# Second block of a two-block model on Trainium2: x kept token-major, norms per token tile

## The reference, cut to what matters

```python
def rmsnorm(x, g):
    xf = x.astype(jnp.float32)
    y = xf * lax.rsqrt(jnp.mean(xf * xf, axis=-1, keepdims=True) + EPS)
    return (y * g.astype(jnp.float32)).astype(x.dtype)

# end of the first block, layer 1
x = x + g2[:, None, :] * hier_moe(h, ...)      # 16 experts, 2 of them per token

for l in range(DEPTH):                         # second block, DEPTH = 2
    h = rmsnorm(x, norm_mix_pre[l])
    proj = h @ w_in[l]                         # retention, short conv, long conv, gates
    ...
    merged = gates[:, :, 0] * y_ret + gates[:, :, 1] * y_sc + gates[:, :, 2] * y_cf
    x = x + rmsnorm(merged @ w_o[l], norm_mix_post[l])

    h = rmsnorm(x, norm_ffn_pre[l])
    up = causal_dwconv(h @ w_up[l], ffn_conv_w[l])
    gate, val = jnp.split(up, 2, axis=-1)      # 2816 features each
    f = (jax.nn.silu(gate) * val) @ w_down[l]
    x = x + rmsnorm(f, norm_ffn_post[l])
```

## Time and profile before

| | us |
|---|---|
| median of 3 runs | 3486.62 (3484.47 to 3488.95) |
| the profiled execution, its own time | 3486.04 |
| its span, first to last instruction | 3484.3 |
| TensorE busy (matmul) | 3043.4, 87% of the span |
| VectorE busy | 2129.5, 61% |
| ScalarE busy | 1261.6, 36% |
| POOL busy | 466.0, 13% |
| mean granted TensorE clock | 0.932 |

### The profile page before, as it was taken

The page is one execution under the profiler, slowest core; times in us unless marked ns, Lnnn a source line. Parts: engine busy times, 40 slices in busy tenths (PEclk is TensorE's granted clock), DMA queues, the critical chain, the costliest instruction groups (busy, mean ns, idle before and its releaser), DMA issues. The chain is left out here.

```text
span 3484.3 us, 32354 instructions
## 1 busy us (share of the span) xinstructions
PE 3043.4 (87%) x12460; PEld 2334.5 (67%) x12460; DVE 2129.5 (61%) x2371; ACT 1261.6 (36%) x1417; POOL 466.0 (13%) x118
## 2 busy tenths in 40 slices
PE   2699698887888787999899996999969999969997
PEld 2334476665767665777677874787858777758876
DVE  5544779978788845997565743665055565266621
ACT  3224257643211113886322233443132223234422
POOL 1100100002400010000000002344410000124432
PEclk9879899998989897999999998999989999989998
DMA  4200459962200002996221221222222222212221
GB/s 189 109 0 23 171 217 412 412 239 97 88 10 22 16 25 73 350 361 254 101 85 62 97 85 61 85 96 85 96 79 97 73 85 85 85 52 97 98 91 60
DMA packets 87148, 420.01 MB, mean 121 GB/s; under 512 B 9651, under 2 KB 14899, under 8 KB 58732
## 3 DMA queue, kind: packets, MB, share of 16 engines
q1 hardware_dynamic: 81260, 376.32, 29.8%
q10 hardware_dynamic: 5760, 41.95, 3.1%
HBM read 416.14 MB, written 2.10 MB: 120 GB/s over the span
## 5 line engine op out<-in xcount | busy, mean ns | idle before, releaser
L221 PE MATMUL psum<-h_high,weights_low 128*128 128x512 f32 x2016 | 799.8, 397 | 58.3 <-DVE h_low L340 56.6
L184 POOL TENSOR_TENSOR weights_low<-weights_raw,weights_high 128x2048 fp32r<-128x2048 f32 x99 | 461.1, 4657 | 2883.3 <-ACT weights_high L180 2883.3
L222 PE MATMUL psum<-h_high,weights_high 128*128 128x512 f32 x2016 | 793.8, 394 | 0.0
L223 PE MATMUL psum<-h_low,weights_high 128*128 128x512 f32 x2016 | 792.9, 393 | 0.0
L180 ACT ACTIVATE weights_high<-weights_raw 128x2048 fp32r<-128x2048 f32 x167 | 319.7, 1915 | 801.5 <-PE psum L223 750.1
L221 PEld LDWEIGHTS psum<-h_high,weights_low 128*128 128x128 f32 x2016 | 384.7, 191 | 159.2 <-issue 78.4
L222 PEld LDWEIGHTS psum<-h_high,weights_high 128*128 128x128 f32 x2016 | 384.3, 191 | 81.3 <-issue 1.4
L223 PEld LDWEIGHTS psum<-h_low,weights_high 128*128 128x128 f32 x2016 | 384.0, 190 | 81.2
L340 DVE TENSOR_TENSOR weights_low<-weights_raw,weights_high 128x2048 fp32r<-128x2048 f32 x68 | 155.8, 2292 | 280.1 <-ACT weights_high L180 280.1
L1329 DVE TENSOR_TENSOR weights_low<-more_raw,weights_high 128x1024 fp32r<-128x1024 f32 x168 | 202.0, 1220 | 13.2 <-ACT weights_high L1000 8.5
L1000 ACT ACTIVATE weights_high<-more_raw 128x1024 fp32r<-128x1024 f32 x168 | 178.5, 1062 | 71.1 <-PE psum L1146 32.9
(11 more groups left out here) (410 smaller groups left out, 4726.3 us busy)
## 6 DMA issues: line engine op xcount, KB each, us to landing
weights_raw<-in_moe SPq DMA_DIRECT2D x168, 512.0 KB, 5.9
more_raw<-in_moe SPq DMA_DIRECT2D x168, 512.0 KB, 6.2
weights_raw<-in_w_mix SPq DMA_DIRECT2D x68, 1024.0 KB, 4.8
weights_raw<-in_w_up SPq DMA_DIRECT2D x44, 1024.0 KB, 4.8
mod_weights<-in_ada_w ACTq DMA_DIRECT2D x40, 1024.0 KB, 8.0
weights_raw<-in_w_down SPq DMA_DIRECT2D x22, 1024.0 KB, 4.9
weights_raw<-in_hy_w_in SPq DMA_DIRECT2D x12, 1024.0 KB, 4.8
mod_weights<-in_ada_w SPq DMA_DIRECT2D x8, 1024.0 KB, 15.8
```

The source lines that it names most:

```text
L184: self.nc.gpsimd.tensor_tensor(self.low[:, g % 2, :], self.raw[:, g % 2, :], self.high[:, g % 2, :].bitcast(F32), ALU.subtract).then_inc(s ...
L221: nc.tensor.matmul(out, w[1], rhs[0], start=start, stop=False)
L222: nc.tensor.matmul(out, w[0], rhs[0], start=False, stop=False)
L223: return nc.tensor.matmul(out, w[0], rhs[1], start=False, stop=stop)
```

## The change

From the last expert phase on, x is token-major: `m.X` has 128 tokens on the partitions, and `token_tile(m, t)` is the 1024 features of token tile t. The expert return, the output projection and ffn-down take a token tile as the stationary operand and stream the weights (or expert results), so their PSUM result is token-major too, two banks for each of four token tiles. The norms then sum along the free axis, per tile, with `accum_out`, and the root is one number for each partition. `tail_act`, `tail_pe` and `tail_dve` do, tile by tile, the norm behind the projection, the residual, the next norm, the transposes of h back to feature-major, and its high and low parts; the norms at the head of `phase_mix` and `phase_ffn_up` are gone. The gains come as rows of 1024, spread over the partitions, by DMA (`load_rows`). In the expert phase x is flipped by 32 transposes, and the gate is spread to a row by 8 matmuls, within the routing. The ScalarE step that makes the next phase's first high part stands behind `tail_act` there. The last phase stores each token tile as it is ready. The loops of `phase_ffn_down` are unrolled, and buffers are laid out anew (`moe_front`, `Gs`, `hT`).

```diff
+            if pre is not None:
+                load_rows(sp, s, pre_row, (pre,))
...
+            def x_tokens(first, end):
+                for c in range(first, end):
+                    act.wait_ge(s.x_flip, c + 1)
+                    nc.scalar.activation(m.X[:, c, :], m.psum[:, c % 4, :], ACT.Copy).then_inc(s.x_token, 1)
+            if pre is not None:
+                x_tokens(0, 4)
             act.wait_ge(s.m2, 1)
             nc.scalar.activation(EL[:, 1, :, :], EL[:, 1, :, :], ACT.Exp).then_inc(s.e2, 1)
+            if pre is not None:
+                x_tokens(4, KC)
+                act.wait_ge(s.gate_spread, 1)
+                nc.scalar.activation(gate_row[:, :], token_psum(m, 3), ACT.Copy).then_inc(s.gate_out, 1)
             highs(2)
             for c in range(KC):
                 act.wait_ge(s.gathered, c + 1)
...
+            if pre is not None:
+                tail_act(nc, act, m, s, post=False)
             if following is not None:
...
+            if pre is not None:
+                pe.wait_ge(s.tok_low, KC)
+                for c in range(KC):
+                    if c >= 4:
+                        pe.wait_ge(s.x_token, c - 3)
+                    for t in range(TT):
+                        mm = nc.tensor.transpose(m.psum[:, c % 4, t * P:(t + 1) * P], m.X[:, c, t * P:(t + 1) * P],
+                                                 m.const("ident"))
+                    mm.then_inc(s.x_flip, 1)
+                pe.wait_ge(s.m1, 1)
+                for c in range(KC):
+                    mm = nc.tensor.matmul(token_psum(m, 3)[:, c * P:(c + 1) * P], gate[:, c:c + 1].broadcast_to([P, P]),
+                                          m.const("ident"), start=True, stop=True)
+                mm.then_inc(s.gate_spread, 1)
...
+            def back_tokens(t, slots):
+                for half in range(2):
+                    for k in slots:
+                        for y in (xl, xh):
+                            mm = nc.tensor.matmul(m.psum[:, 2 * t + half, :], rows[:, k, t * P:(t + 1) * P],
+                                                  y[:, k, 4 * half:4 * half + 4, :].rearrange("p c n -> p (c n)"),
+                                                  start=(k == 0 and y is xl), stop=(k == SLOTS - 1 and y is xh))
+                return mm
             pe.wait_ge(s.slot_rows, 1)
             pe.wait_ge(s.y_ready, SLOTS - 1)
+            if pre is not None:
+                for t in range(2):
+                    back_tokens(t, range(SLOTS - 1))
+                pe.wait_ge(s.y_ready, SLOTS)
+                for t in range(2):
+                    back_tokens(t, range(SLOTS - 1, SLOTS)).then_inc(s.y_tile, 1)
+                for t in range(2, TT):
+                    back_tokens(t, range(SLOTS)).then_inc(s.y_tile, 1)
+                tail_pe(nc, pe, m, s)
+                return
             for c in range(4):
                 back(c, c, range(SLOTS - 1))
...
+def token_tile(m, t):
+    return m.X[:, :, t * P:(t + 1) * P]
...
+def tail_y_root(nc, act, m, s, t):
+    act.wait_ge(s.y_tile, t + 1)
+    nc.scalar.activation(m.hT[:, t, :], token_psum(m, t), ACT.Square, accum_out=m.stats[:, t:t + 1]).then_inc(s.y_summed, 1)
+    act.wait_ge(s.y_summed, t + 1)
+    nc.scalar.activation(m.stats[:, 4 + t:5 + t], m.stats[:, t:t + 1], ACT.Sqrt, bias=m.const("eps"), scale=1.0 / D)\
+        .then_inc(s.y_root, 1)
+def tail_x_root(nc, act, m, s, t):
+    act.wait_ge(s.x_ready, t + 1)
+    nc.scalar.activation(by_feature(m.hT[:, t, :]), token_tile(m, t), ACT.Square, accum_out=m.stats[:, 8 + t:9 + t])\
+        .then_inc(s.x_summed, 1)
+    act.wait_ge(s.x_summed, t + 1)
+    nc.scalar.activation(m.stats[:, 12 + t:13 + t], m.stats[:, 8 + t:9 + t], ACT.Sqrt, bias=m.const("eps"), scale=1.0 / D)\
+        .then_inc(s.x_root, 1)
...
+def tail_high(nc, act, m, s, t):
+    act.wait_ge(s.h_flip, t + 1)
+    nc.scalar.activation(m.Hh[:, :, t * P:(t + 1) * P], by_feature(token_psum(m, t)), ACT.Copy).then_inc(s.t_high, 1)
...
+def tail_act(nc, act, m, s, post=True, pre=True):
+    for step in range(TT + 2):
+        if post and step < TT:
+            tail_y_root(nc, act, m, s, step)
+        if pre and 1 <= step <= TT:
+            tail_x_root(nc, act, m, s, step - 1)
+        if pre and step >= 2:
+            tail_high(nc, act, m, s, step - 2)
...
+def tail_pe(nc, pe, m, s):
+    for t in range(TT):
+        pe.wait_ge(s.h_tok, t + 1)
+        for c in range(KC):
+            mm = nc.tensor.transpose(token_psum(m, t)[:, c * P:(c + 1) * P], m.hT[:, t, c * P:(c + 1) * P], m.const("ident"))
+        mm.then_inc(s.h_flip, 1)
...
+def tail_dve(nc, dve, m, s, link, row, pre=None, gated=False, keep=True):
+    stt, tt = nc.vector.scalar_tensor_tensor, nc.vector.tensor_tensor
+    def residual(t):
+        h = m.hT[:, t, :]
+        if gated:
+            dve.wait_ge(s.y_tile, t + 1)
+            link(tt(h, token_psum(m, t), row, ALU.mult))
+        else:
+            dve.wait_ge(s.y_root, t + 1)
+            link(nc.vector.reciprocal(m.stats[:, 4 + t:5 + t], m.stats[:, 4 + t:5 + t]))
+            link(stt(h, token_psum(m, t), m.stats[:, 4 + t:5 + t], row, ALU.mult, ALU.mult))
+        out = token_tile(m, t) if keep else by_feature(h)
+        tt(out, token_tile(m, t), by_feature(h), ALU.add).then_inc(s.x_ready, 1)
+    def normed(t):
+        dve.wait_ge(s.x_root, t + 1)
+        link(nc.vector.reciprocal(m.stats[:, 12 + t:13 + t], m.stats[:, 12 + t:13 + t]))
+        stt(by_feature(m.hT[:, t, :]), token_tile(m, t), m.stats[:, 12 + t:13 + t], by_feature(pre), ALU.mult, ALU.mult)\
+            .then_inc(s.h_tok, 1)
+    def low(t):
+        dve.wait_ge(s.t_high, t + 1)
+        at = slice(t * P, (t + 1) * P)
+        low_part(nc, m.Hl[:, :, at], by_feature(token_psum(m, t)), m.Hh[:, :, at]).then_inc(s.t_ready, 1)
+    for step in range(TT + 2):
+        if step < TT:
+            residual(step)
+        if pre is not None and 1 <= step <= TT:
+            normed(step - 1)
+        if pre is not None and step >= 2:
+            low(step - 2)
 
 
 def phase_mix_out(nc, m, ph, ring, d, layer, following):
 
     n = 4
...
             for u in range(n):
-                unit_products(nc, pe, ring, u, m.Hs, m.psum, k_ready=h_tiles(pe, s) if u == 0 else None)
-            post_norm_pe(nc, pe, m, s, m.raw)
+                pe.wait_ge(s.g_ready, 2 * u + 2)
+                w = [x.rearrange("p (k m) -> p k m", k=2) for x in ring.parts(pe, u)]
+                for t in range(TT):
+                    for half in range(2):
+                        for k in range(2):
+                            c = 2 * u + k
+                            mm = split_matmul(nc, m.psum[:, 2 * t + half, :], [x[:, c, t * P:(t + 1) * P] for x in (Gh, Gl)],
+                                              [x[:, k, half * S:(half + 1) * S] for x in w], c == 0, c == KC - 1)
+                    if u == n - 1 and t < TT - 1:
+                        mm.then_inc(s.y_tile, 1)
+                if u < n - 1:
+                    mm.then_inc(ring.used, 1)
+                else:
+                    mm.then_inc(s.y_tile, 1)
+            pe.wait_ge(s.y_tile, TT)
+            pe.sem_inc(ring.used, 1)
+            tail_pe(nc, pe, m, s)
 
         @block.scalar
         def _(act):
             for c in range(KC):
-                nc.scalar.activation(m.Hh[:, c, :], m.merged[:, c, :], ACT.Copy).then_inc(s.h_high, 1)
-            ring.make_high(act, 1)
-            act.wait_ge(s.h_ready, KC)
-            for u in range(n):
-                ring.products(act, u)
-                for c in (2 * u, 2 * u + 1):
-                    post_norm_tile(nc, m, s, c, m.merged, m.raw, m.param("mix_post", KC, layer * KC))
-                if u < n - 1:
-                    ring.make_high(act, u + 2)
-            post_norm_root(nc, act, m, s)
+                nc.scalar.activation(Gh[:, c, :], m.merged[:, c, :], ACT.Copy).then_inc(s.g_high, 1)
+                if c == 1:
+                    ring.make_high(act, 1)
+            for u in range(n - 1):
+                ring.make_high(act, u + 2)
+            tail_act(nc, act, m, s)
 
         @block.vector
...
-            norm_pe(nc, pe, m, s)
-            pe.wait_ge(s.root, 1)
-            streamed_products(nc, pe, ring, n, m.Hs, m.psum, s.read_out, k_ready=h_tiles(pe, s))
+            streamed_products(nc, pe, ring, n, m.Hs, m.psum, s.read_out)
...
+            if last_layer:
+                load_rows(sp, s, rows, (d.rows[4 * layer + 3, :, :],))
+                for t in range(TT):
+                    sp.wait_ge(s.x_ready, t + 1)
+                    sp.dma_start(d.out[t, :, :], m.hT[:, t, :]).then_inc(s.stored, 16)
+                sp.wait_ge(s.rows_here, 16)
+                sp.wait_ge(s.stored, 16 * TT)
+            else:
+                load_rows(sp, s, rows, (d.rows[4 * layer + 3, :, :], d.rows[4 * layer + 4, :, :]))
+                sp.wait_ge(s.rows_here, 32)
```

236 lines of the change are left out of this document (108 added, 128 removed).

## The result

The changed kernel takes 3433.02 us (median of four runs, 3431.02 to 3435.19) against 3487.57 for the kernel before beside it (3484.47 to 3488.95): a ratio of 0.9845, with a 95% interval of 0.9833 to 0.9857. The profiled execution took 3431.02 us with a span of 3428.8, so 55.0 less than the profiled one of before. The forecast was 3437, 48.8 less.

What follows compares the result with a forecast made beforehand. Bound by TensorE in its phases and, between them, by a serial chain on VectorE and ScalarE. Terms -44.3 - 14.1 + 4.4 + 3.5 + 0.5 + 1.2 = -48.8 us take 3486.0 to 3437.2; range 3424 to 3454.

Steps and rivals of the forecast that it cites:

- The three tails: Behind both output projections and layer 0's ffn-down: gap 18.5 us against 33.8, 32.2 and 33.85, saving 44.3 us.
- The end: End of program: only the residual per tile and a 512 KB store remain; E+9.0 instead of E+23.1, saving 14.1 us.
- Behind the expert phase: After the last expert phase: first high part queued behind ScalarE's tail, gap E+21.2 against 16.8, costing 4.4 us.
- Routing: Last expert phase: transposes and gate spread enter TensorE's queue ahead of the rank matmuls, shifting them by 3.5 us.
- The row in the expert stream: SP waits for a 512 KB row with weight loads queued behind; buffers cover nearly all, cost 0.5 us (0 to 3).
- Heads of the output projections: First product waits for two tiles of merged instead of one: 0.6 us twice, costing 1.2 us.
- Unrolled ffn-down: Loops of ffn-down become straight code, as the mix phase is already; no cost.
- Pace: Products with the token tile stationary run as fast as the dense stream, as the v units do; no cost.
- rival 1: Token-major products of output projection and ffn-down go at the slower branch pace: 9.5 us more, 3447; chance 0.10.
- Rival 2: ScalarE's table switch delays each tail's first root by 1.38 us, in three tails and the end: 3443; chance 0.05.
- Rival 3: Flips keep TensorE at 2.4 GHz through tails and next starts: 3 x 3.0 = 9 us less, 3428; chance 0.12.
- Rival 4: Loading the stationary token tile isn't hidden in the 1440 products: 271 us more, 3708, slower than before; chance 0.03.

## Why the prediction was right

The path was read right: from last product to first, with VectorE's queue as what sets a tail's length. Term by term:

- *The three tails.* -44.3 forecast, -45.9 measured. The model put tile 3's addition at E+9.3, which is where it is. What was too long by half a microsecond is the part behind it: eight transposes take 1.97 us, not 2.3, since the nearest rows were runs of four, whose first and last weigh more. The accumulating square was feared at up to 1.5 us and takes 1.03 plus a read of the accumulator of 0.19. The gap of 17.90 lies just under the 18 to 19 that was named as the sign. Two parts of the saving are now separate numbers, which the prediction didn't split: 8.2 for the overlap, 5.5 to 6.2 for the narrow roots.
- *The end.* E+8.5 against E+9.0: the addition ends at E+5.4 as forecast, the last store takes 3.0 us and not the 3.5 of the nearest row.
- *Behind the expert phase.* The mechanism, named in the prediction, was shown by its removal (19.3 to 14.0). The growth was 2.5 instead of 4.4, because the tail's last Copy ends at E+12.6, not E+14.2. The 16 transposes of tiles 0 and 1 came straight behind the last product at full clock.
- *Routing.* +1.1 against +3.5, the term that was sized worst. The 32 transposes took 3.71 us (0.115 each) where 4.7 was taken, the spread 1.95 instead of 2.3. Above all the prediction moved the rank matmuls as they were, and the new work in front of them kept the clock up: they take 1.8 us where they took 3.6 at half, and end at 1349.0 where 1350.5 was named. The step that failed is that a moved block keeps its duration. The timeline of TensorE after, whose last line is the start of the ranks:

```profile
1341.81 3.71 PE L1126 MATMUL psum<-consts,x 128*128 128x128 f32 x32 [0.81 <-DVE tok_low L1285]
1345.36 1.95 PE L1131 MATMUL psum<-consts,mod 128*128 128x128 f32 x16
1347.15 0.29 PE L1136 MATMUL psum<-group,consts 128*128 128x16 f32 x2
```

- *The row in the expert stream.* At least 1.4 by the kernels with the wait moved, against 0.5 (0 to 3). The wait delays the next load by 5.9 us (8.4 instead of 2.5 behind the row's issue), and the buffers cover 4.5 of them. The stage grew by only 0.75, so 0.65 came back elsewhere in it, which no run places.
- *Heads of the output projections.* +1.0 against +1.2.
- *Unrolled ffn-down.* Nothing, as forecast, though no run separates it: from the first product of ffn-up to the last of ffn-down the phases take 370.6 us in both layers before, and 370.0 and 372.2 after.
- *Pace.* Nothing, as forecast, and here by luck. It took the v units as evidence that the form is fast. The form is neither fast nor slow: the place in memory decides, and 32 bytes more would have made rival 1 true. Nothing in the prediction made sure of the place.
- *Rivals.* Rival 2 falls: the root starts 1.29 us after its table load starts. The Trainium skill, ScalarE: Activation LUTs, section What ACT_TABLE_LOAD costs, adds a drain of about 1380 ns to the load; the load's 1.28 us agree, and no drain is seen in these tails. Rival 3 (the clock stays up) is true for little more than the first tile's transposes; the kernel with all fillers shows its price, 3.5 us a boundary (13.9 at four) where 3.0 was given. Rival 4 falls with the spacing of 0.227.
- *Not foreseen.* Mix of layer 0 is 2.0 us shorter in the first profile (416.5 against 418.5), but 418.0 in the second. Between these two the clock came back 2.9 and 5.7 us behind the first product, which is 1.4 of the 1.5; it is scatter of the clock and not shown to be an effect of the change. The 2.2 of the two mix phases are all but cancelled by 1.8 in other stretches. The 6.2 us between 48.8 and 55.0 lie for the most part in the two over-sized terms of the expert phase (1.9 and 2.4) and in the tails (1.6).

## What to carry to other kernels

A norm between two matmul phases costs what lies between the last product and the first. Tile it so that the work on a tile runs under the product of the next, and give each row its root as one number on its partition: here the first was worth 8.2 us a boundary and the second 5.5 to 6.2. When work is moved into a tail, look at what is queued behind it on each engine, the next phase's first operand part above all; one swap of two calls turned a loss of 2.5 us into a gain of 2.8. And give TensorE something to do in the pauses of such a tail, in all of them: with every pause filled the phase behind started at the full clock, and no gap grew. Where one pause was left open, the filler behind it ran at the half level and held the first product up by 0.6 us.

## What the hardware showed that was not expected

- A product with 512 moving columns, its operands in fp32r, takes 0.2267 or 0.2333 us, according to whether one of its operands lies at one place or 32 bytes further. It was shown in both directions: by moving the stationary operand, which slowed output projection and ffn-down, and by moving the moving one, which sped up the branch products.
- The pauses of a tail, up to 3.2 us behind a projection and 5.3 behind the experts, between bursts of 1 to 2 us, took the granted clock to 0.50, and after the products resumed it stayed there for 2.8 to 5.8 us in the eight tails of two profiles. With filler transposes in every pause it stayed at 1.00 through all four tails (the longest pause left was 1.3 us).
- A sum taken along with a ScalarE activation adds an instruction of 0.19 us (ACTIVATION_READ_ACCUMULATOR) behind each.
- A VectorE operation of 512 columns that takes 0.74 us took 2.02 when it started beside a GpSimd subtraction of 2048 columns; it ended 0.55 us behind the subtraction. The subtraction took 4.86 us there, as in the kernel before at the same place, and 4.60 at the end of the expert phase.
